# Softmax weights turned in 32x32 blocks by VectorE and through DRAM, in place of TensorE transposes

## The chip, the cores and the metric

The kernel runs on one core of a Trainium2 chip. The metric is the device time of one execution in microseconds, the median of several runs. The kernel before takes 755.2 us (754.77 to 755.24 in three runs). TensorE, VectorE (DVE in the rows), ScalarE (ACT), GpSimd (POOL) and SyncE (SP) each work through a queue of their own, in order, and wait for each other on semaphores; a DMA is issued by one of these queues and runs on the core's 16 DMA engines.

## What is computed

One layer of a hybrid encoder over two batches, of 1024 and of 512 tokens, 1024 wide. An RMS norm and one input projection feed three mixers: latent attention with 4 heads, centred pooling, and gated linear attention. Each mixer's output is multiplied by the SiLU of its gates, the three are joined, projected by `w_out` and added to the input; a last RMS norm follows. The change is in the attention:

```python
def attend(blk):
    qn, qr = blk
    s = (jnp.einsum('bqhd,bkhd->bhqk', qn, k_nope, preferred_element_type=jnp.float32)
         + jnp.einsum('bqhr,bkr->bhqk', qr, k_rope, preferred_element_type=jnp.float32))
    p = jax.nn.softmax(s * MLA_SCALE, axis=-1)
    return jnp.einsum('bhqk,bkhd->bqhd', p.astype(v.dtype), v)
```

## The kernel before

All products of float32 operands are made as three products of a high and a low part (`product`: high x high, high x low, low x high), both parts in the type fp32r. A split is a copy to fp32r (high) and a subtraction (low).

The program has three phases that pass through the same five queues: `phase_front` (norm, input projection, pooling, linear attention), `phase_mla_attend` (attention), `phase_output` (gates, output projection, last norm). The attention has 4 heads x 12 query tiles of 128 = 48 steps (`STEPS`). A tile of the long batch meets 1024 keys (8 blocks of 128, "long"), one of the short batch 512 ("short"); the first eight tiles of a head are long, the last four short. The work is written as a hand-made software pipeline: every engine runs the loop `for m in range(STEPS + GATHER_LAG)` and does in iteration m the scores of tile m and later stages of earlier tiles, by the constants `TURN_LAG, VALUES_LAG, OUTPUT_LAG, GATHER_LAG = 2, 4, 5, 6`:

- TensorE, `scores(m)`: five products per 512 keys into PSUM banks 0 to 3 (two tiles in turn).
- VectorE: the row's maximum (`a_top`) and from it `a_bias`; ScalarE: the exponential into `a_weights` in SBUF, with its sum.
- TensorE, `turn(m)` (line 1994), two steps later: eight or four 128x128 transposes into banks 4 and 5.
- ScalarE takes the high part `a_turned_hi` from there, VectorE subtracts for `a_turned_lo`, a bank of four blocks each time.
- TensorE, `values(p)`, for a pair p of tiles (2p, 2p+1): tokens x turned weights, 24 products of 256 columns for a long pair, 12 for a short one; ScalarE and VectorE split the result (`a_latent_hi`, `a_latent_lo`); TensorE multiplies it by the head's value weights (`output(p)`); VectorE scales it by the reciprocal of the sum and puts it into `mla_mixed` (gather).

In iterations 5, 7 and 9 of a head, `project` makes the next head's queries. In the last head SyncE loads the eight 512 KB rows of `w_out`, GpSimd splits them, and the first tile's mix and gates are made ready; `multiply_first` puts the first tile's mix products between the last steps, `multiply(0, s)` in `phase_output` does the rest of tiles 0 and 1. GpSimd does nothing else in the attention.

## Time and profile before

| | us |
|---|---|
| median of three runs | 755.2 |
| the profiled execution | 754.49 |
| its span | 752.7 |
| TensorE busy | 740.5 |
| VectorE, ScalarE, GpSimd busy | 413.5, 310.1, 219.5 |

The profile is of one execution. Its span runs from the first to the last instruction; 1.8 us of the execution's time lie outside. The busy time of TensorE includes the overlap of products in flight: what one costs is the distance from its start to the next one's. The attention's first product of scores starts at 399.7 us, the output phase's product of tile 1 at 624.2, the last matmul ends at 746.4.

How the rows further down are read. A row of busy time by stretch has the stretch, its length, then busy time and (x instructions) of PE, PEld (TensorE's weight loads, which overlap its matmuls), DVE, ACT and POOL, the granted clock of TensorE as a share of full speed, the mean busy share of the DMA engines and the GB/s that they moved. A row in order of time has start, duration, engine, line, operation, output<-input, shapes and, in brackets, the idle time ahead of it with what ended it. A row of a group has busy time, mean ns of one | idle time ahead of it, with what ended that. A row of DMA issues has KB of one and median us from issue to landing.

### The profile page before, as it was taken

What the parts mean: (1) busy time and instruction counts of PE and PEld (TensorE: products, weight loads), DVE (VectorE), ACT (ScalarE), POOL (GpSimd) and SP (SyncE); (2) the same over time, 40 slices, a digit from 0 to 9 for tenths busy, and PEclk for the clock granted to TensorE, in tenths of its full rate; (3) what the DMA queues carried; (4) which work ended last, traced back from release to release, by engine and by line L of the source; (5) the groups of instructions that cost most, each with busy time, mean ns of one, the idle gap of its engine ahead of it and who ended that gap; (6) DMA issues with size and microseconds to landing.
All of it is one profiled execution on the core that took longest, in us unless ns stands there. A gap on an engine that the chain in (4) does not pass through costs nothing.

```text
span 752.7 us, 14593 instructions
## 1 busy us (share of the span) xinstructions
PE 740.5 (98%) x6024; PEld 625.1 (83%) x6024; DVE 413.5 (55%) x742; ACT 310.1 (41%) x536; POOL 219.5 (29%) x262
## 2 busy tenths in 40 slices
PE   8999999999999999999999999999999999999996
PEld 6997878878888888888887988898898888888885
DVE  6745867376576542026265667667667754433232
ACT  6653544434423422323225545455546643232221
POOL 3223236366556513122400000000009704322320
PEclk9999999999999999999999999999999999999998
DMA  7603021001112133230143000000043035564441
GB/s 255 184 23 88 28 97 57 30 31 40 62 71 88 71 113 118 99 82 13 63 168 112 16 15 14 15 16 15 15 152 128 0 96 177 190 195 151 143 152 56
DMA packets 40623, 64.70 MB, mean 86 GB/s; under 512 B 4434, under 2 KB 23378, under 8 KB 40563
## 3 DMA queue, kind: packets, MB, share of 16 engines
q1 hardware_dynamic: 34272, 49.61, 20.6%
q10 hardware_dynamic: 6290, 14.23, 4.9%
q8 instruction: 45, 0.74, 0.4%
q14 instruction: 16, 0.12, 0.1%
HBM read 43.58 MB, written 19.27 MB: 83 GB/s over the span
## 4 chain that ended last, share of the span: by engine, by line
PE 93%; DVE 3%; ACT 1%; POOL 1%; issue 1%; DMA 0%; DVEq 0%; POOLq 0%
PE psum L78 24%; PE psum L80 23%; PE psum L79 23%; PE psum L1994 5%; PE psum L1521 3%; PE psum L1985 2%; PE psum L1986 2%; PE psum L1360 2%; PE psum L1254 1%; DVE g_state L1062 1%; PE psum L1390 1%; PE psum L1415 1%; PE psum L2014 1%; PE psum L1315 1%; PE psum L1384 1%
## 5 line engine op out<-in xcount | busy, mean ns | idle before, releaser
L78 PE MATMUL psum<-h_hi,z_w_hi 128*128 128x512 f32 x384 | 155.5, 405 | 1.4 <-POOL z_w_lo L805 1.4
L80 PE MATMUL psum<-h_hi,z_w_lo 128*128 128x512 f32 x384 | 149.9, 390 | 0.0
L79 PE MATMUL psum<-h_lo,z_w_hi 128*128 128x512 f32 x384 | 149.8, 390 | 0.0
L78 PEld LDWEIGHTS psum<-h_hi,z_w_hi 128*128 128x128 f32 x384 | 72.1, 188 | 18.0 <-POOL z_w_lo L805 1.8
L80 PEld LDWEIGHTS psum<-h_hi,z_w_lo 128*128 128x128 f32 x384 | 72.1, 188 | 15.6
L79 PEld LDWEIGHTS psum<-h_lo,z_w_hi 128*128 128x128 f32 x384 | 72.2, 188 | 14.3 <-issue 0.7
L78 PE MATMUL psum<-o_w_hi,o_m_hi 128*128 128x512 f32 x184 | 72.6, 394 | 0.0
L80 PE MATMUL psum<-o_w_hi,o_m_lo 128*128 128x512 f32 x184 | 72.3, 393 | 0.0
L79 PE MATMUL psum<-o_w_lo,o_m_hi 128*128 128x512 f32 x184 | 72.2, 392 | 0.0
L1863 ACT ACTIVATE a_weights<-psum,a_bias,mla_q_scale 128x1024 f32<-128x1024 f32 (+1 forms) x48 | 51.1, 1065 | 46.9 <-DVE a_bias L1924 46.7
L805 POOL TENSOR_TENSOR z_w_lo<-z_w_raw,z_w_hi 128x1024 fp32r<-128x1024 f32 x17 | 41.8, 2460 | 95.6 <-ACT z_w_hi L501 93.5
L1812 POOL CAST o_w_hi<-o_w_raw 128x512 fp32r<-128x512 f32 x16 | 9.3, 608 | 194.9 <-DMA o_w_raw<-in_w_out_dram 194.9
L1921 DVE TENSOR_REDUCE a_top<-psum 128x1 f32<-128x1024 f32 (+1 forms) x48 | 50.1, 1043 | 26.8 <-PE psum L1986 26.8
L1877 ACT ACTIVATE a_turned_hi<-psum 128x512 fp32r<-128x512 f32 x80 | 44.2, 596 | 33.7 <-PE psum L1994 32.8
L1076 DVE COPY_PREDICATED g_attn<-g_level_mask,psum 128x256 f32<-128x256 int32 x72 | 32.3, 449 | 38.4 <-ACT g_attn L675 36.3
L1948 DVE TENSOR_TENSOR a_turned_lo<-psum,a_turned_hi 128x512 fp32r<-128x512 f32 x80 | 51.9, 682 | 2.6 <-ACT a_turned_hi L1877 2.6
L2238 DVE TENSOR_TENSOR o_y<-psum,o_x_in 128x512 f32<-128x512 f32 x24 | 16.4, 689 | 53.1 <-PE psum L80 53.1
L80 PE MATMUL psum<-a_turned_hi,mla_tokens_lo 128*128 128x256 f32 x160 | 45.3, 283 | 0.0
L79 PE MATMUL psum<-a_turned_lo,mla_tokens_hi 128*128 128x256 f32 x160 | 45.3, 283 | 0.0
L78 PE MATMUL psum<-a_turned_hi,mla_tokens_hi 128*128 128x256 f32 x160 | 45.2, 282 | 0.0
L514 ACT ACTIVATE z_gate<-psum 128x512 f32<-128x512 f32 x24 | 14.3, 597 | 71.6 <-PE psum L80 71.6
L1994 PE MATMUL psum<-ident,a_weights 128*128 128x128 f32 x320 | 43.6, 275 | 0.0
(252 smaller groups left out, 1520.1 us busy)
## 6 DMA issues: line engine op xcount, KB each, us to landing
z_w_raw<-in_w_z_dram SPq DMA_DIRECT2D x17, 512.0 KB, 3.5
n_x_in<-in_x_dram SPq DMA_DIRECT2D x12, 512.0 KB, 4.1
gates_scratch<-z_gate ACTq DMA_DIRECT2D x24, 256.0 KB, 2.1
o_x_in<-in_x_dram SPq DMA_DIRECT2D x12, 512.0 KB, 3.6
out_dram<-o_y ACTq DMA_DIRECT2D x11, 512.0 KB, 3.2
o_w_raw<-in_w_out_dram SPq DMA_DIRECT2D x8, 512.0 KB, 8.7
rope_scratch<-p_rope_split SPq DMA_DIRECT2D x12, 256.0 KB, 2.6
a_q_rope<-rope_scratch SPq DMA_DIRECT2D x48, 64.0 KB, 1.9
```

Source lines behind the costliest of these rows:

```text
L78: nc.tensor.matmul(out, a_hi, b_hi, start=first, stop=False)
L79: nc.tensor.matmul(out, a_hi, b_lo, start=False, stop=False)
L80: return nc.tensor.matmul(out, a_lo, b_hi, start=False, stop=last)
L805: nc.gpsimd.tensor_tensor(w_lo[:, o % 2, :], raw_of(o)[:, :], w_hi[:, o % 2, :].bitcast(F32), ALU.subtract).then_inc(w_lo_ready, 1)
L1076: nc.vector.copy_predicated(attn[:, t % 2, :, :], level_mask[:, n, :].bitcast(mybir.dt.int32).unsqueeze(1).broadcast_to([P, HEADS, CHUNK]) ...
L1521: mm = nc.tensor.matmul(psum[:, i, part * UNIT:(part + 1) * UNIT], (w_lo if kind == W_LOW else w_hi)[:, o, c], (h_lo if kind == H_LOW else ...
L1863: nc.scalar.activation(weights[:, m % SLOTS, 0:count * P].rearrange("p (a k) -> p a k", k=BLK), psum[:, banks, :], ACT.Exp, bias=bias[:, m ...
L1877: nc.scalar.activation(turned_hi[:, p % 2, 4 * n:4 * n + 4, (tile % 2) * P:(tile % 2 + 1) * P], psum[:, 4 + item % 2, :].rearrange("p (k q ...
L1921: nc.vector.tensor_reduce(top[:, m:m + 1], psum[:, banks, :], mybir.AxisListType.XY, ALU.max)\
L1948: nc.vector.tensor_tensor(turned_lo[at], psum[:, 4 + item % 2, :].rearrange("p (k q) -> p k q", k=4), turned_hi[at].bitcast(F32), ALU.subt ...
L1994: mm = nc.tensor.transpose(psum[:, 4 + item % 2, k * P:(k + 1) * P], weights[:, m % SLOTS, (4 * n + k) * P:(4 * n + k + 1) * P], ident[:, :])
L2238: nc.vector.tensor_tensor(y[:, s, cols], psum[:, 1 - s + 2 * half, :], x_in[:, s, cols], ALU.add)\
```

## The change

- The exponential stays in PSUM (written over the scores). Three pairs of banks hold scores, in place of two.
- VectorE transposes each 32x32 block of the tile from PSUM into `a_spread` in SBUF, arranged by groups of 32 keys. That leaves the partition groups in the wrong place.
- A pass through DRAM exchanges them: ScalarE's queue stores a tile (512 or 256 KB) in iteration m+1, and when both tiles of a pair are stored SyncE issues four loads of 32 partitions each (1 KB or 512 bytes a row) into `a_turned_lo`.
- ScalarE copies that to fp32r for `a_turned_hi` in iterations 2p+3; the low part is subtracted in place, by GpSimd for tiles 0 to 35, 36, 38, 40 and 42, by VectorE for the others.
- The values product comes one step later, so do output and gather. The transposes on TensorE go.
- The next head's queries are made in iterations 8, 9 and 10, in spare banks of the scores.
- The loads of `w_out` are spread over pairs 17 to 22; ScalarE copies the high part of four of its rows (iterations 46 and 48); the mix products of tile 0 stand in iterations 48 and 49, its eight head products in iteration 50 (`multiply_heads`).
- In `phase_front` the first block after the early ones does all products with the weights' high part first and waits for the low part only then.

```diff
@@ TensorE, phase_front.project
+                if i == EARLY and first == 0:
+                    pe.wait_ge(w_hi_ready, o + 1)
...
+                if i == EARLY:
+                    steps = [(HIGH, first, h_hi, w_hi), (H_LOW, first, h_lo, w_hi)]
+                    if last == KT:
+                        steps.append((W_LOW, 0, h_hi, w_lo))
@@ the tables
-TURN_LAG, VALUES_LAG, OUTPUT_LAG, GATHER_LAG = 2, 4, 5, 6
-PROJECT_AT = {5: 0, 7: 1, 9: 2}
+VALUES_LAG, OUTPUT_LAG, GATHER_LAG = 5, 6, 7
+PROJECT_AT = {8: 0, 9: 1, 10: 2}
+W_OUT_LOADS = {17: (4, 5), 18: (6,), 19: (7,), 20: (0, 1), 21: (2,), 22: (3,)}
+W_HI_BY_SCALAR = {46: (0, 1), 48: (2, 3)}
...
+def high_parts_at(m):
+
+    if m % 2 and 1 <= m - 2 < STEPS:
+        return [m - 3, m - 2]
+    return []
@@ SyncE
+            for p in range(PAIRS):
...
+                for n in range(2):
+                    sp.wait_ge(spread_stored[(2 * p + n) % SLOTS], 16 * ((2 * p + n) // SLOTS) + 16)
+                if p >= 2:
+                    sp.wait_ge(values_done, p - 1)
+                for g in range(4):
+                    keys = slice(g * SPREAD, (g + 1) * SPREAD)
+                    sp.dma_start(turned_lo[keys, p % 2, 0:2 * count].bitcast(F32).rearrange("p (x e) -> p x e", x=8),
+                                 rows[p % 3].rearrange("t (a p) (g e) -> g p (t a) e", a=4, g=4)[g])\
+                      .then_inc(turned_loaded[p % 2], 16)
@@ ScalarE
+            def store_spread(m):
+                count, p = keys_of(m), m // 2
+                act.wait_ge(transposed, m + 1)
...
+                act.dma_start(spread_dram[count][p % 3, m % 2], spread[:, m % SLOTS, 0:count])\
+                  .then_inc(spread_stored[m % SLOTS], 16)
...
-                nc.scalar.activation(weights[:, m % SLOTS, 0:count * P].rearrange("p (a k) -> p a k", k=BLK),
-                                     psum[:, banks, :], ACT.Exp, bias=bias[:, m:m + 1],
+                nc.scalar.activation(psum[:, banks, :], psum[:, banks, :], ACT.Exp, bias=bias[:, m:m + 1],
...
+            def take_high(m):
...
+                nc.scalar.activation(turned_hi[part], turned_lo[part].bitcast(F32), ACT.Copy).then_inc(turned_hi_ready, 1)
...
             for m in range(STEPS + GATHER_LAG):
+                if 1 <= m <= STEPS:
+                    store_spread(m - 1)
                 if m < STEPS:
                     exponentials(m)
...
+                for tile in high_parts_at(m):
+                    take_high(tile)
@@ VectorE
+            def transpose(m):
...
+                nc.vector.transpose(spread[:, m % SLOTS, 0:count].rearrange("p (g j e) -> p j g e", g=4, e=SPREAD),
+                                    psum[:, banks, :].rearrange("p b (j g e) -> p (b j) g e", g=4, e=SPREAD))\
@@ GpSimd
+            def take_low(m):
+                pool.wait_ge(turned_hi_ready, m + 1)
+                part = (slice(None), m // 2 % 2, portion(m))
+                nc.gpsimd.tensor_tensor(turned_lo[part], turned_lo[part].bitcast(F32), turned_hi[part].bitcast(F32), ALU.subtract)\
+                  .then_inc(pool_low, 1)
@@ TensorE
-            def turn(m):
...
-                if m >= 2:
-                    pe.wait_ge(exp_done, m - 1)
+                if m >= SLOTS:
+                    pe.wait_ge(transposed, m - 2)
...
+                if m == HEADS_PRODUCTS_STEP:
+                    multiply_heads()
```

How the order of instructions moves, at three places. ScalarE, in the middle of a head's long tiles, before (`a_turned` is the semaphore of TensorE's transposes):

```order
L1877 ACTIVATE a_turned_hi_5117<-psum 128x4x128 [waits a_turned,a_values_done]
L1877 ACTIVATE a_turned_hi_5117<-psum 128x4x128 [waits a_turned]
L1863 ACTIVATE a_weights_5121,a_total_5124<-psum,a_bias_5123,mla_q_scale_67 128x1024 [waits a_turned,a_bias_ready] x2
L1891 ACTIVATE a_latent_hi_5119<-psum 128x256 [waits a_values_done]
L1877 ACTIVATE a_turned_hi_5117<-psum 128x4x128 [waits a_turned] x2
L1877 ACTIVATE a_turned_hi_5117<-psum 128x4x128 [waits a_turned,a_values_done]
L1877 ACTIVATE a_turned_hi_5117<-psum 128x4x128 [waits a_turned]
L1863 ACTIVATE a_weights_5121,a_total_5124<-psum,a_bias_5123,mla_q_scale_67 128x1024 [waits a_turned,a_bias_ready] x2
```

ScalarE at the same place, after (`a_transposed` counts VectorE's block transposes, `a_turned_loaded` the loads of a pair, `a_spread` goes to DRAM):

```order
L1957 ACTIVATE a_turned_hi_5118<-a_turned_lo_5119 128x1024 [waits a_turned_loaded1]
L1937 DMA spread_scratch1024<-a_spread_5122 128x1024 [waits a_transposed]
L1944 ACTIVATE psum,a_total_5125<-psum,a_bias_5124,mla_q_scale_67 128x1024 [waits a_bias_ready]
L1970 ACTIVATE a_latent_hi_5120<-psum 128x256 [waits a_values_done]
L1937 DMA spread_scratch1024<-a_spread_5122 128x1024 [waits a_turned_loaded0,a_transposed]
L1944 ACTIVATE psum,a_total_5125<-psum,a_bias_5124,mla_q_scale_67 128x1024 [waits a_bias_ready]
L1957 ACTIVATE a_turned_hi_5118<-a_turned_lo_5119 128x1024 [waits a_values_done,a_turned_loaded0]
L1957 ACTIVATE a_turned_hi_5118<-a_turned_lo_5119 128x1024 [waits a_turned_loaded0]
L1937 DMA spread_scratch1024<-a_spread_5122 128x1024 [waits a_transposed]
```

The exponential no longer waits for TensorE; a store stands ahead of each exponential, and the two high parts of a pair stand after every second one, ahead of the next store.

VectorE, long tiles, before:

```order
L1943 RECIPROCAL a_share_5125<-a_total_5124 128x1 [waits a_exp_done]
L1948 TENSOR_TENSOR a_turned_lo_5118<-psum,a_turned_hi_5117 128x4x128 [waits a_turned_hi_ready] x2
L1921 TENSOR_REDUCE a_top_5122<-psum 128x1 [waits a_scores_done]
L1924 TENSOR_SCALAR a_bias_5123<-a_top_5122,mla_q_scale_67 128x1 [waits a_top_ready]
L1943 RECIPROCAL a_share_5125<-a_total_5124 128x1 [waits a_exp_done]
L1948 TENSOR_TENSOR a_turned_lo_5118<-psum,a_turned_hi_5117 128x4x128 [waits a_turned_hi_ready] x2
L1921 TENSOR_REDUCE a_top_5122<-psum 128x1 [waits a_scores_done]
```

VectorE at the same place, after:

```order
L2016 TENSOR_REDUCE a_top_5123<-psum 128x1 [waits a_scores_done]
L2019 TENSOR_SCALAR a_bias_5124<-a_top_5123,mla_q_scale_67 128x1 [waits a_top_ready]
L1997 STREAM_TRANSPOSE a_spread_5122<-psum 128x8x4x32 [waits a_spread_stored1,a_exp_done]
L2032 RECIPROCAL a_share_5126<-a_total_5125 128x1
L2016 TENSOR_REDUCE a_top_5123<-psum 128x1 [waits a_scores_done]
L2019 TENSOR_SCALAR a_bias_5124<-a_top_5123,mla_q_scale_67 128x1 [waits a_top_ready]
L2024 COPY a_share_row_74<-psum 128x256 [waits a_output_done]
```

The low part of the turned weights is gone, and between one tile's bias and the next tile's maximum stands the block transpose, which waits for that tile's exponential and for a free slot of `a_spread`.

ScalarE, at the end of the last head, after (tiles 42 to 46; `o_first_step` counts GpSimd's steps on the first tile's mix and gates):

```order
L1957 ACTIVATE a_turned_hi_5118<-a_turned_lo_5119 128x1024 [waits a_values_done,a_turned_loaded1]
L1957 ACTIVATE a_turned_hi_5118<-a_turned_lo_5119 128x1024 [waits a_turned_loaded1]
L1907 ACTIVATE o_first_hi_75<-o_mix_first_73 128x512 [waits o_gate_turned,o_first_step]
L1937 DMA spread_scratch512<-a_spread_5122 128x512 [waits a_transposed]
L1944 ACTIVATE psum,a_total_5125<-psum,a_bias_5124,mla_q_scale_67 128x512 [waits a_bias_ready]
L1970 ACTIVATE a_latent_hi_5120<-psum 128x256 [waits a_values_done]
L1902 ACTIVATE o_gate_first_72<-o_gate_first_72 128x512 [waits o_first_step]
L1913 ACTIVATE o_w_hi0_95<-o_w_raw0_79 128x512 [waits w_out_loaded0]
L1913 ACTIVATE o_w_hi1_96<-o_w_raw0_79 128x512
L1913 ACTIVATE o_w_hi2_97<-o_w_raw1_80 128x512 [waits w_out_loaded1]
```

The copy of the first mix stands between the high parts of tiles 42 and 43 and the store of tile 45; four copies of output weights stand between the exponentials of tiles 46 and 47.

## Rows read from the trace of the kernel before

**Rows 1.** Busy time by stretch: one whole head of the attention
```profile
432.65:486.72 54.07, 54.07 (x351) 48.17 (x349) 37.36 (x77) 28.00 (x53) 0.00 (x0) 1.00 0.06 15
```

**Rows 2.** TensorE, instructions in order of time, 480 to 492 us
```profile
480.03 0.40 PE L78 MATMUL psum<-mla_ckv_hi,a_q_hi 128*128 128x512 f32 x1
...
483.68 0.28 PE L78 MATMUL psum<-a_turned_hi,mla_tokens_hi 128*128 128x256 f32 x1
...
486.56 1.04 PE L1994 MATMUL psum<-ident,a_weights 128*128 128x128 f32 x8
```

**Rows 3.** The page's costliest groups: the transposes of the weights
```profile
L1994 PE MATMUL psum<-ident,a_weights 128*128 128x128 f32 x320 | 43.6, 275 | 0.0
```

**Rows 4.** VectorE and ScalarE in order of time, the first tile
```profile
402.34 1.23 DVE L1921 TENSOR_REDUCE a_top<-psum 128x1 f32<-128x1024 f32 x1 [1.12 <-PE psum L1986]
403.60 0.22 DVE L1924 TENSOR_SCALAR a_bias<-a_top,mla_q_scale 128x1 f32<-128x1 f32 x1
403.85 1.21 ACT L1863 ACTIVATE a_weights<-psum,a_bias,mla_q_scale 128x1024 f32<-128x1024 f32 x1 [3.35 <-DVE a_bias L1924]
404.95 0.19 ACT L1863 ACTIVATION_READ_ACCUMULATOR a_weights<-psum,a_bias,mla_q_scale 128x1 f32 x1
```

**Rows 5.** Groups by line and form, VectorE, 400 to 612 us
```profile
L1937 DVE TENSOR_TENSOR a_latent_lo<-psum,a_latent_hi 128x256 fp32r<-128x256 f32 x23 | 9.8, 424 | 24.6 <-ACT a_latent_hi L1891 24.6
```

**Rows 6.** ScalarE and its DMA queue in order of time, 178 to 180 us
```profile
178.52 0.60 ACT L514 ACTIVATE z_gate<-psum 128x512 f32<-128x512 f32 x1 [4.67 <-PE psum L80]
178.53 0.35 ACTq L547 DMA_DIRECT2D gates_scratch<-z_gate  x1
179.01 1.05 ACT L501 ACTIVATE z_w_hi<-z_w_raw 128x1024 fp32r<-128x1024 f32 x1
```

**Rows 7.** Groups by line, GpSimd, whole span
```profile
L805 POOL TENSOR_TENSOR z_w_lo<-z_w_raw,z_w_hi 128x1024 fp32r<-128x1024 f32 x17 | 41.8, 2460 | 95.6 <-ACT z_w_hi L501 93.5 <-DVE n_x_norm L1107 2.1
L1817 POOL TENSOR_TENSOR o_w_lo<-o_w_raw,o_w_hi 128x512 fp32r<-128x512 f32 x16 | 20.3, 1290 | 0.0
```

**Rows 8.** DMA issues alone in 736:745, 178:182, 115:125; KB, us to landing
```profile
out_dram<-o_y ACTq DMA_DIRECT2D x1, 512.0 KB, 2.6
...
gates_scratch<-z_gate ACTq DMA_DIRECT2D x1, 256.0 KB, 2.1
...
z_w_raw<-in_w_z_dram SPq DMA_DIRECT2D x1, 512.0 KB, 3.3
```

**Rows 9.** Busy time by stretch: DMA engines full, 512-byte rows, then 4 KB
```profile
559.00:560.00 1.00, 1.00 (x8) 0.83 (x7) 0.23 (x1) 0.00 (x0) 0.00 (x0) 1.00 1.21 339
...
565.00:568.00 3.00, 3.00 (x19) 2.57 (x18) 2.15 (x5) 1.89 (x5) 3.00 (x5) 1.00 1.03 408
```

**Rows 10.** ScalarE, VectorE, TensorE in order of time, 615 to 625 us
```profile
615.88 1.28 ACT L2164 ACT_TABLE_LOAD   x1
...
619.31 1.06 ACT L2164 ACTIVATE o_gate_second<-o_gate_second 128x1024 f32<-128x1024 f32 x1 [2.15 <-DMA o_gate_second<-gates_scratch]
...
621.84 0.63 ACT L2171 ACTIVATE o_m_hi<-mla_mixed 128x512 fp32r<-128x512 f32 x1 [1.47 <-POOL mla_mixed L2127]
...
622.51 1.10 DVE L2224 TENSOR_TENSOR o_m_lo<-mla_mixed,o_m_hi 128x512 fp32r<-128x512 f32 x1 [4.19 <-ACT o_m_hi L2171]
...
624.21 0.40 PE L78 MATMUL psum<-o_w_hi,o_m_hi 128*128 128x512 f32 x1
```

**Rows 11.** Busy time by stretch: around TensorE's last matmul
```profile
746.00:748.00 2.00, 0.38 (x2) 0.00 (x0) 0.69 (x1) 0.72 (x2) 0.06 (x1) 1.00 0.00 0
748.00:750.00 2.00, 0.00 (x0) 0.00 (x0) 1.21 (x2) 0.00 (x0) 0.68 (x2) 0.71 0.00 0
```

**Rows 12.** TensorE in order of time, 56 to 60 us
```profile
58.65 0.50 PE L78 MATMUL psum<-h_hi,z_w_hi 128*128 128x512 f32 x1 [1.39 <-POOL z_w_lo L805]
```

**Rows 13.** VectorE in order of time, 632 to 648 us
```profile
634.44 2.30 DVE L2244 SCALAR_TENSOR_TENSOR o_y<-o_y,o_rstd,o_g_row 128x1024 f32<-128x1024 f32 x1 [3.45 <-POOL o_rstd L2142]
...
640.89 1.28 DVE L2244 SCALAR_TENSOR_TENSOR o_y<-o_y,o_rstd,o_g_row 128x1024 f32<-128x1024 f32 x1
```

334 lines of the change are left out of this document (193 added, 141 removed).

## The prediction

> **What bounds the kernel now.** I read the busy shares by stretch first. In one head of the attention (12 query tiles, 54.07 us) TensorE is busy all of the time at the full granted clock, VectorE 37.4 us and ScalarE 28.0 us of it, GpSimd not at all, and the DMA engines 6% [rows 1]. So TensorE's own work sets the head, and the reader is to see that the other queues have room on paper. Then the order of TensorE's work: from 480.03 to 483.68 stand 16 products over 512 columns, 0.228 us each, and from there to 486.56 stand 24 over 256 columns, 0.12 us each [rows 2]. The transposes that the change removes hold TensorE for 43.6 us in all, 10.9 us a head [rows 3]. A long pair of tiles (8 key blocks) is left with 20 x 0.228 + 24 x 0.12 + about 0.6 for the output product = 8.0 us of TensorE, a head with some 43 us in place of 54.
>
> **What replaces them.** A tile's weights now go through seven hands: exponential on ScalarE, block transpose on VectorE, a store on ScalarE's queue, four loads on SyncE's queue, the high part on ScalarE, the low part on GpSimd, the values product. Each hand has time; what I have to ask is whether two of them form a circle. They form two.
>
> **Circle 1, through DRAM.** The order of ScalarE's instructions shows it: store of tile 2p+2, exponential, high parts of tiles 2p and 2p+1, and only then the store of tile 2p+3. The two high parts wait for the loads of pair p, and the loads of pair p+1 wait for the store of tile 2p+3. So one pair cannot take less than: one high part, a store, the loads. The price of each:
> - High part over 1024 columns out of SBUF: a ScalarE copy of that size takes 1.05 us, and the next starts some 0.1 earlier: 0.95. A DMA issue on ScalarE's queue starts together with the copy ahead of it (178.52 and 178.53) [rows 6], so only the first of the two high parts is in the circle. That is a choice: were both in it, it would be 0.95 longer.
> - Store of 512 KB: 2.6 us from issue to landing, 256 KB 2.1 [rows 8].
> - SyncE's wake-up: 0.1, an estimate.
> - Loads: a load of 0.52 MB alone takes 3.3 us [rows 8]; at the 408 GB/s of full DMA engines with 4 KB rows [rows 9] 1.3 of these are data, 2.0 are fixed. The new rows are 1 KB, which no stretch shows full; 512-byte rows ran at 339 GB/s [rows 9]. I take 360, between them: 1.05 MB in 2.9 us (2.6 to 3.1 by the ends). In the same time the store of the next tile is under way, another 0.52 MB, 1.3 us. Loads: 2.0 + 2.9 + 1.3 = 6.2 us. Ends: 4.6 if the store falls beside them and the rate is the higher, 7.5 if reads and writes disturb each other.
>
> Sum for a long pair: 0.95 + 2.6 + 0.1 + 6.2 = 9.9 us. With a short tile's store in it 9.2; a short pair (half the bytes) 0.5 + 2.1 + 0.1 + 4.2 = 6.9.
>
> **Circle 2, VectorE and ScalarE.** VectorE's order per tile is now maximum, bias, block transpose; the transpose waits for the exponential of the same tile, and the maximum of the next tile is queued behind it. From maximum to exponential 1.51 us, exponential with its sum 1.29 [rows 4], the transpose, and 0.1 for two handovers. The trace has no block transpose. Below I bound it by the maximum over the same 1024 elements of PSUM, 1.23 us, above by the longest VectorE row over 1024, 2.30 us [rows 13]; I take 1.23, as it is the row that reads the same banks. A tile: 4.13; a pair with the low part of the latents (0.42 [rows 5]): 8.7 us. (The Trainium skill, Vector Engine (DVE) Microarchitecture Reference, section 3.8 on the reshape front-end, says that the 32x32 array is pipelined to one element per cycle and lane, so an estimate from that page would be little over the maximum's time, and the sum would be the same; no run here shows it yet.)
>
> So circle 1 sets long pairs at 9.9, circle 2 the pairs in which short tiles are loaded while long ones are computed, 8.7. Neither is under TensorE's 8.0. GpSimd has two low parts of 2.46 us a pair [rows 7] and is no bound; they are late, but SyncE and ScalarE don't wait for them. TensorE waits for them at the values product, in one idle block of 2 us a pair, with nothing but its own later work queued behind.
>
> **When the pairs end.** First maximum at 402.34 [rows 4]; exponential done 405.1, transpose 406.4, second tile 4.1 later 410.6; store 413.2; loads 419.5. From there to the loads of pair 21: 11 pairs of 9.9, 4 of 9.2, 3 of 6.9, 3 of 8.7 = 192.5, that is 612.0. The weights of the output product, 4.2 MB, are now loaded between these; 10 us of DMA time in six gaps, of which I let 2 us through: 614.0.
>
> **The last pairs.** Counted from these loads (0). High parts 0 to 2, low part on GpSimd 1.0 to 3.5, two multiplications of the gates to 5.5; ScalarE's copy of the first mix, which stands ahead of the store of tile 45, waits for that (5.5 in place of 1.0). VectorE is behind the same copy, so tile 46 has its exponential at 8.8; then 2.4 us of weight copies on ScalarE; tile 47's exponential 13.1, transpose 13.8, store 15.9, loads 19.8, high parts 20.9. GpSimd's last splits of the output weights, 4 x 2 x 1.29 [rows 7] and the gates, end at 23.4; TensorE waits for them and does the eight products of tile 0 (5.5, to 28.9), values and outputs of the last two pairs (to 34.9). Tile 1 then needs a table load of 1.28, the gates' Silu and GpSimd's multiplication (619.31 to 621.84, 2.5), a copy of 0.63 and a split of about 0.7 [rows 10], partly beside the last output: product of tile 1 at 39. Before, it starts at 624.21 [rows 10]. Now: 614.0 + 39 = 653.0, later by 28.8.
>
> **The rest.** From tile 1's first product to the last matmul 746.4 - 624.2 = 122.2, then 6.3 to the end of the span, both unchanged. The reordered first products after the early blocks wait for the high half alone: the 1.39 us wait at 58.65 goes [rows 12]; behind it TensorE is busy, so it is worth 1.4. The clock: it stood at 1.00 in 746 to 748, in which the last matmul ended, and at 0.71 (partly at the lower level of 1.2 GHz) in the next two microseconds [rows 11]. TensorE will wait 3.6 and 4.2 us in the last pairs and 2 us in each pair; within the pairs its slack of 1.9 covers a slower start, at the end I add 2.0 (ends 0 and 5.5, the eight products at half speed). Sum: 752.7 + 28.8 - 1.4 + 2.0 = 782.1 of span; with the profiled execution's 1.8 outside its span 783.9; the median of the runs shown lies 0.7 above that execution: 784.6, so **785 us**.
>
> **A rule that bears on it.** At 634.44 a VectorE instruction with two SBUF inputs took 2.30 us beside a GpSimd multiplication, and 1.28 at 640.89 without one [rows 13]. (The Trainium skill, SBUF — State Buffer, section "SBUF: two separate sides", calls the shared port pair an exclusive lock between GpSimd and VectorE instructions with two SBUF inputs; by that rule the trace agrees.) The 40 new low parts on GpSimd read SBUF, but VectorE's work in the first three heads reads PSUM; only its eight low parts in the last head meet them, 1 us each at most, of which the last may count: within the range.
>
> **Rivals.**
> 1. The loads are hidden (the store beside them costs nothing, fixed parts overlap): circle 2 sets all long pairs at 8.7. 11 x 1.2 + 4 x 0.5 = 15 less, last pairs 4 less: **766**. For it: the DMA engines have 5.6 us of data in 9.9. Against: every load and store alone already makes 8.3.
> 2. The transpose runs at the upper bound, 1.07 longer a tile: circle 2 is 10.8. 11 x 0.9 + 4 x 1.6 + 3 x 2.1 + the tail's 2: **809**. Reads and writes that disturb each other (loads 7.5) give about the same, 805.
> 3. On the other side: TensorE stays the bound. It does if a pair's circles are both under 8.0, that is the loads under 4.3 us and the transpose under 0.9. Then 43.6 goes, the longer fill (some 5) and last pairs (some 14) give back 19: **730**. For it: in a head TensorE is busy all of the time [rows 1], and the removed work is its own. Against: the prices above; it decides at 8.0 us a long pair. Break-even with before is at about 8.3.
> 4. The clock stays at its lower level during the heads: TensorE needs 16 us a pair and becomes the bound: about 870. Against: two microseconds of waiting near 58 left it at 1.00; a slow TensorE has no more waits.
>
> **Chances.** My forecast 0.46, rival 1 0.20, rival 2 0.13, rival 3 0.17, rival 4 0.01, about equal to before 0.03. Below and above 0.2% (about what a measurement of this kernel can tell from no change): faster 0.17, same 0.03, slower 0.80. The range, which holds forecast and rivals 1 and 2: 757 to 813.
>
> **What the profile after would show.** Right: TensorE at 80 to 85% in the heads, waiting at the first values product for GpSimd's low part; ScalarE's high part waiting for the loads of a_turned_lo; long pairs 9.9 us apart; loads landing 6 us after the store; in the last pairs a wait of the mix copy for GpSimd. Wrong: ScalarE waiting for the bias instead (rival 1 or 2, told apart by the transpose's duration), or TensorE without waits (rival 3). What would break the forecast: a DMA issue that runs ahead of both high parts (a pair 0.95 shorter, 14 us in all), or loads of 1 KB rows well off 360 GB/s.

## The result, and the profile after

The changed kernel takes **822.4 us** (817.9 to 823.2 in four runs) against 755.1: ratio 1.088 (1.087 to 1.090). The prediction said 785, with 757 to 813 as the range. It had the sign and not the size: 67 us lost where 30 were forecast.

The profiled execution took 821.9, its span 820.1. One whole head, from the first maximum to the next head's, answers to [rows 1]; columns as there:

```profile
462.60:524.00 61.40, 48.83 (x270) 41.79 (x269) 35.90 (x70) 26.83 (x45) 24.70 (x13) 0.94 0.60 184
```

54 us have become 61.4, TensorE is busy for 80% of them, and the DMA engines, at 6% before, stand at 60%. On the page, in place of the transposes of [rows 3], stand VectorE's transposes and GpSimd's low parts ("..." marks lines left out):

```profile
L1849 POOL TENSOR_TENSOR a_turned_lo<-a_turned_lo,a_turned_hi 128x1024 fp32r<-128x1024 f32 (+1 forms) x40 | 80.9, 2041 | 183.2 <-ACT a_turned_hi L1957 183.2
...
L1997 DVE STREAM_TRANSPOSE a_spread<-psum 128x1024 f32<-128x1024 f32 (+1 forms) x48 | 51.4, 1070 | 65.0 <-ACT psum L1944 64.8
...
L2104 PE MATMUL psum<-ident,a_share 128*128 128x128 f32 x48 | 11.9, 338 | 58.5 <-DVE a_latent_lo L2035 58.5
```

Most of TensorE's waiting in the attention (58.5 us) is at one instruction, the first of an output product, for the low part of the latents; I had put it at the values product, which waits for a low part of the weights once, for 7.8 us. What stands behind it all is in the chain of work that ended last, here through two long pairs (start, us, what):

```profile
482.88 2.62 DMA spread_scratch<-a_spread
485.50 0.02 SPq L1813
485.52 0.03 issue
485.55 0.30 SPq L1816
...
486.88 6.80 DMA a_turned_lo<-spread_scratch
493.68 0.02 issue
493.71 0.01 ACT a_turned_hi L1957
493.71 2.61 DMA spread_scratch<-a_spread
...
497.72 6.78 DMA a_turned_lo<-spread_scratch
504.50 0.02 issue
504.52 0.01 ACT a_turned_hi L1957
504.53 2.62 DMA spread_scratch<-a_spread
```

Store, four issues, loads, store: no engine computes in this chain. ScalarE in order of time shows how the circle closes:

```profile
493.71 1.06 ACT L1957 ACTIVATE a_turned_hi<-a_turned_lo 128x1024 fp32r<-128x1024 f32 x1 [3.29 <-DMA a_turned_lo<-spread_scratch]
493.71 0.33 ACTq L1937 DMA_DIRECT2D spread_scratch<-a_spread  x1
494.67 1.05 ACT L1957 ACTIVATE a_turned_hi<-a_turned_lo 128x1024 fp32r<-128x1024 f32 x1
495.62 1.16 ACT L1944 ACTIVATE psum<-psum,a_bias,mla_q_scale 128x1024 f32<-128x1024 f32 x1
```

The store of the odd tile starts together with the first high part, 0.03 us behind the landing of the loads at 493.68. It stands behind two high parts in the order and is delayed by neither, but it is delayed by their wait.

Where the time went, by VectorE's maxima of tiles 0, 36 and 47 (402.34 in [rows 4], the others from the same view). Before:

```profile
559.77 1.22 DVE L1921 TENSOR_REDUCE a_top<-psum 128x1 f32<-128x1024 f32 x1 [0.98 <-PE psum L1986]
...
604.23 0.68 DVE L1921 TENSOR_REDUCE a_top<-psum 128x1 f32<-128x512 f32 x1
```

After:

```profile
400.89 1.23 DVE L2016 TENSOR_REDUCE a_top<-psum 128x1 f32<-128x1024 f32 x1 [1.04 <-PE psum L2080]
...
587.03 1.23 DVE L2016 TENSOR_REDUCE a_top<-psum 128x1 f32<-128x1024 f32 x1 [3.21 <-PE psum L2080]
...
656.95 0.68 DVE L2016 TENSOR_REDUCE a_top<-psum 128x1 f32<-128x512 f32 x1
```

e13, in the last column, is the run without the pass and without the low parts of the first three heads (see the experiments).

| us | before | after | e13 |
|---|---|---|---|
| start to tile 0 | 402.3 | 400.9 | 401.1 |
| tile 0 to 36, three heads | 157.4 | 186.1 | 151.0 |
| tile 36 to 47, last head | 44.5 | 69.9 | 53.9 |
| tile 47 to the end of the span | 148.5 | 163.2 | 163.5 |
| span | 752.7 | 820.1 | 769.5 |

### The profile page after: what moved, and what is told of

It is laid out like the page before. It is cut to its first block, busy times and chain, and to the rows that moved or that the text cites. A ratio compares the mean times of both kernels' runs of the same rounds, so it can differ in the third digit from the quotient of the medians.

```text
span 820.1 us, 14085 instructions
## 1 busy us (share of the span) xinstructions
PE 731.5 (89%) x5704; PEld 608.6 (74%) x5704; DVE 419.2 (51%) x718; ACT 309.8 (38%) x512; POOL 299.1 (36%) x294
## 4 chain that ended last, share of the span: by engine, by line
PE 65%; DMA 19%; DVE 4%; ACT 3%; SPq 3%; POOL 3%; issue 2%; DVEq 0%; POOLq 0%; ACTq 0%
PE psum L78 18%; PE psum L80 17%; PE psum L79 17%; DMA a_turned_lo<-spread_scratch 14%; DMA spread_scratch<-a_spread 5%; PE psum L1535 4%; SPq L1816 3%; PE psum L1374 2%; PE psum L1254 1%; DVE g_state L1062 1%; PE psum L1404 1%; PE psum L1429 1%; ACT psum L1944 1%; ACT a_turned_hi L1957 1%; DVE a_spread L1997 1%
## 5 line engine op out<-in xcount | busy, mean ns | idle before, releaser
L78 PE MATMUL psum<-h_hi,z_w_hi 128*128 128x512 f32 x376 | 152.4, 405 | 0.0
L1849 POOL TENSOR_TENSOR a_turned_lo<-a_turned_lo,a_turned_hi 128x1024 fp32r<-128x1024 f32 (+1 forms) x40 | 80.9, 2041 | 183.2 <-ACT a_turned_hi L1957 183.2
L80 PE MATMUL psum<-h_hi,z_w_lo 128*128 128x512 f32 x376 | 146.7, 390 | 0.0
L79 PE MATMUL psum<-h_lo,z_w_hi 128*128 128x512 f32 x376 | 146.6, 390 | 0.0
L1997 DVE STREAM_TRANSPOSE a_spread<-psum 128x1024 f32<-128x1024 f32 (+1 forms) x48 | 51.4, 1070 | 65.0 <-ACT psum L1944 64.8
L78 PEld LDWEIGHTS psum<-h_hi,z_w_hi 128*128 128x128 f32 x376 | 70.6, 188 | 15.9 <-issue 0.7
L1944 ACT ACTIVATE psum<-psum,a_bias,mla_q_scale 128x1024 f32<-128x1024 f32 (+1 forms) x48 | 49.4, 1029 | 85.6 <-DVE a_bias L2019 83.2
L1957 ACT ACTIVATE a_turned_hi<-a_turned_lo 128x1024 fp32r<-128x1024 f32 (+1 forms) x48 | 41.3, 907 | 63.1 <-DMA a_turned_lo<-spread_scratch 63.1
L2104 PE MATMUL psum<-ident,a_share 128*128 128x128 f32 x48 | 11.9, 338 | 58.5 <-DVE a_latent_lo L2035 58.5
L2016 DVE TENSOR_REDUCE a_top<-psum 128x1 f32<-128x1024 f32 (+1 forms) x48 | 49.5, 1032 | 13.1 <-PE psum L2080 13.1
L2104 PEld LDWEIGHTS psum<-ident,a_share 128*128 128x128 f32 x48 | 5.8, 161 | 66.3 <-DVE a_share L2032 63.1
L78 PEld LDWEIGHTS psum<-o_w_hi,o_m_hi 128*128 128x128 f32 x184 | 35.5, 193 | 16.0 <-issue 7.9
```

Of the source, the lines that this page charges most:

```text
L78: nc.tensor.matmul(out, a_hi, b_hi, start=first, stop=False)
L79: nc.tensor.matmul(out, a_hi, b_lo, start=False, stop=False)
L80: return nc.tensor.matmul(out, a_lo, b_hi, start=False, stop=last)
L1849: nc.gpsimd.tensor_tensor(turned_lo[part], turned_lo[part].bitcast(F32), turned_hi[part].bitcast(F32), ALU.subtract)\
L1944: nc.scalar.activation(psum[:, banks, :], psum[:, banks, :], ACT.Exp, bias=bias[:, m:m + 1], scale=keep.q_scale[:, tile:tile + 1], accum_o ...
L1957: nc.scalar.activation(turned_hi[part], turned_lo[part].bitcast(F32), ACT.Copy).then_inc(turned_hi_ready, 1)
```

## The experiments

Times are medians; ratios are to runs of the kernel before on the same chip, with their 95% interval. A store counts from its issue to its last landing, the loads from the first issue to the last landing; a pair's time is the distance between the last landings of its loads and of the loads before. Differences of under 5 us between two kernels are to be read with care: the changed kernel's own four runs lie between 817.9 and 823.2. In the cuts of code "..." marks lines left out.

### What the pass costs

**No low part.** GpSimd's subtraction left out:

```diff
@@ GpSimd
-            for m in range(LAST_HEAD):
-                take_low(m)
@@ TensorE, values, first three heads
-                pe.wait_ge(pool_low, sum(m <= tiles[1] for m in POOL_LOW))
+                pe.wait_ge(turned_hi_ready, tiles[1] + 1)
```

> GpSimd's low parts of the turned weights are left out for the first three heads (tiles 0 to 35); the values products take the loaded weights themselves for the low part, so the output is not the reference's. Theory A: the low parts (4.7 us for the two of a long pair) are late for TensorE alone, and a long pair's loads don't wait for its values; 822 less 0 to 4: 820. Theory G: the first long loads behind short tiles (465.55, 526.94 and 590.19, each about 3 us behind the landing of the store) wait for a values product that waits for the low part; then 3 such waits go and the chain behind each is shorter: 812 or less.

Measured 820.6, ratio 1.086 (1.085 to 1.088) against 1.088 (1.087 to 1.090) of the changed kernel. 66.7 us of GpSimd work between 425 and 590 us are gone and nothing clear of the noise follows: they were off the path, as theory A had it.

**No pass, first form.** ScalarE takes the high part from `a_spread` two steps later, no store, no loads, shorter lags:

```diff
-VALUES_LAG, OUTPUT_LAG, GATHER_LAG = 5, 6, 7
+VALUES_LAG, OUTPUT_LAG, GATHER_LAG = 3, 4, 5
...
-                nc.scalar.activation(turned_hi[part], turned_lo[part].bitcast(F32), ACT.Copy).then_inc(turned_hi_ready, 1)
+                nc.scalar.activation(turned_hi[part], spread[:, m % SLOTS, 0:keys_of(m)], ACT.Copy).then_inc(turned_hi_ready, 1)
```

> The pass through DRAM is left out: VectorE's block transposes stay, ScalarE and GpSimd take high and low part from their output in SBUF, two tiles later, and values, output and gather come two steps earlier than in the changed kernel. The partition groups are not exchanged, so the output is not the reference's. Theory A (the pass is what costs): VectorE's loop of 4.34 us a long tile and some 2.9 a short one is left, 32 x 4.34 + 16 x 2.9 = 185 us from 401, then some 30 us of last steps, so tile 1 at about 616 to 624 and the end at 752 (744 to 762). Rival: with the transposes gone TensorE is the bound and the time falls by most of their 43.6 us, 730 or less.

817.7, ratio 1.083 (1.081 to 1.084): both theories missed. I took it for a wait of the experiment's own making and moved latents, output and gather one step back (`LATENT_LAG`, `OUTPUT_LAG`, `GATHER_LAG` = 4, 5, 6):

> As the run without the pass through DRAM, but latents, output and gather one step later behind the values, because there VectorE stood at the latents' low part (490.13, idle 3.07) with the next maximum behind it, and TensorE's values waited for the gather. The output is again not the reference's (no exchange of partition groups). Theory A (the pass is what costs, the run before it had a wait of its own making): 752 (744 to 762). Rival H (the hands around the pass are as slow as the pass: TensorE waits for low parts and latents whatever their source): over 795.

837.4, ratio 1.110 (1.108 to 1.112), worse still. VectorE in order of time shows why:

```profile
490.79 1.25 DVE L1985 STREAM_TRANSPOSE a_spread<-psum 128x1024 f32<-128x1024 f32 x1 [1.36 <-ACT psum L1932]
491.97 0.12 DVE L2020 RECIPROCAL a_share<-a_total 128x1 f32<-128x1 f32 x1
498.25 1.23 DVE L2004 TENSOR_REDUCE a_top<-psum 128x1 f32<-128x1024 f32 x1 [6.17 <-PE psum L2068]
```

With a lag of 3 the low part is made right before the values product that needs it (TensorE idle 4.09 us for it at 489.89), and the next scores stand behind that product; so VectorE idles 6.2 us for scores. The lag of five steps had hidden the low parts, as the run without them shows. The time is over rival H's 795, but by waits that the shorter lags made. Neither run measures the pass.

**No pass, same lags.** The transposes write three pairs' places and everything stands in its old step, on top of the run without low parts:

```diff
-                if m >= SLOTS:
-                    dve.wait_ge(spread_stored[m % SLOTS], 16 * (m // SLOTS))
-                nc.vector.transpose(spread[:, m % SLOTS, 0:count].rearrange("p (g j e) -> p j g e", g=4, e=SPREAD),
+                if m >= 6:
+                    dve.wait_ge(values_done, m // 2 - 2)
+                nc.vector.transpose(turned_lo[:, m // 2 % 3, portion(m)].rearrange("p (g j e) -> p j g e", g=4, e=SPREAD),
```

> As the run without low parts in the first three heads, and the pass through DRAM left out as well: VectorE's block transposes write the place of the loaded weights (three pairs of it), ScalarE takes the high parts from there, and every step stands in the iteration in which it stands in the changed kernel. The output is not the reference's (no exchange, no low parts). Beside the 820.6 of the run without low parts this leaves the pass alone as the difference. Theory A (the pass is what costs): VectorE's loop of 4.4 us a long tile and 2.9 a short one, 401 + 187 + 33 = 621 for tile 1, 752 (744 to 762) at the end. Rival H (in-order waits of TensorE around the pass cost as much without it, as the two runs without exchange and with shorter lags would have it, 817.7 and 837.4): over 790.

771.4, ratio 1.022 (1.020 to 1.023). Against the 820.6 of its partner the pass through DRAM costs **49 us**; and without pass and low parts the kernel is still 16 slower than before. Neither forecast had this: theory A said 744 to 762, rival H over 790. The pass is about three quarters of the loss (49 of 67), not all of it. A head takes 50.5 us there:

```profile
451.10:501.60 50.50, 47.16 (x270) 40.70 (x269) 36.15 (x69) 26.88 (x45) 0.00 (x0) 0.97 0.06 16
```

The transposes freed 10.9 us of TensorE in a head, and with a free exchange 3.5 of them come out (50.5 in place of 54.0). The table above shows the rest: three heads 6.4 faster, last head 9.4 and everything behind it 15.0 slower.

### The loads

**Neighbouring rows, and rows of 4 KB.** The loads' source alone is changed:

```diff
-                 rows[p % 3].rearrange("t (a p) (g e) -> g p (t a) e", a=4, g=4)[g])
+                 rows[p % 3].rearrange("t q (r e) -> (t q r) e", r=4).rearrange("(x g p) e -> g p x e", x=8, g=4)[g])
```

> The four loads of a pair read the same number of rows of 1 KB (512 bytes for short tiles), but rows that lie next to each other in DRAM in place of every fourth one; the weights then reach the wrong partitions, so the output is not the reference's. In the changed kernel a 1 KB packet of the loads takes 65 ns in the mean and 46 in the median. Theory D (the stride of 4 KB in DRAM slows the reads): loads of a long pair 6.3 in place of 8.1, 18 long pairs, about 30 us less, 792. Theory E (size of rows, four issues in a row and the store beside them make the 8.1): within 4 us of 822.

```diff
-                for g in range(4):
-                    keys = slice(g * SPREAD, (g + 1) * SPREAD)
...
+                for n in range(2):
+                    sp.dma_start(turned_lo[:, p % 2, n * count:(n + 1) * count].bitcast(F32), rows[p % 3][n])
```

> The pair is loaded by two transfers of 128 partitions with rows of 4 KB (2 KB for short tiles) in place of four with rows of 1 KB; the same bytes, but without the exchange of partition groups, so the output is not the reference's. Theory E (small rows and four issues cost it): first row in flight 1.0, two times 1.3 of data, 1.3 of the next store and some 1 to land: 5.9 us in place of 8.1; 18 pairs, 40 us less, 782 +- 6. Theory F (the reads wait for the rows just written, or for the latency of DRAM, whatever their size): loads still over 7.5 and the time over 812.

809.1, ratio 1.072 (1.070 to 1.074), and 785.1, ratio 1.039 (1.037 to 1.042). The distance of the rows costs 0.6 us of a long pair's loads (8.1 to 7.5 in the mean of eight), not the 1.8 of theory D; neither theory had the time of 809.1 (792 and 818 to 826), of which the rows' distance makes some 11 in 18 pairs. With rows of 4 KB 5.0 to 5.7 are left, 2.4 to 3.1 less, and the time is in theory E's range (776 to 788). But that comparison is not of the rows alone: the last issue comes 0.41 us behind the first in place of 1.35, and only 0.23 to 0.30 MB of the next store lie beside the loads where it was all of its 0.52. Rows' size, number of issues and the store beside are not told apart by a run; the account below takes them from the queues' busy time.

**Rows joined.** The same exchange with the small pieces on the store's side:

```diff
-                act.dma_start(spread_dram[count][p % 3, m % 2], spread[:, m % SLOTS, 0:count])
+                home = spread_dram[count][p % 3].rearrange("t q n -> (t q n)")\
+                    .rearrange("(g p t a e) -> t a p g e", g=4, p=SPREAD, t=2, a=4)
+                for a in range(4):
+                    act.dma_start(home[m % 2, a], spread[a * SPREAD:(a + 1) * SPREAD, m % SLOTS, 0:count].rearrange("p (g e) -> p g e", g=4))
```

> The same exchange by another layout in DRAM: the store writes pieces of 1 KB (four issues of 32 partitions each), so that the load of a pair is one transfer whose row of 8 KB a partition lies in one piece. Theory E (many small rows and issues on the load's side make it 8.1): loads 5.0 to 5.6 as with rows of 4 KB; the store 3.6 with four issues in place of 2.6; 1.6 us a pair less, 18 pairs, 793 +- 6. Rival: the small pieces cost the same on whichever side they are, 815 or more.

804.6, ratio 1.067 (1.064 to 1.069), 18 us less than the changed kernel, where 787 to 799 and for the rival 815 or more had been expected. The chain through two long pairs:

```profile
482.05 2.42 DMA spread_scratch<-a_spread
...
484.53 6.07 DMA a_turned_lo<-spread_scratch
...
491.97 2.36 DMA spread_scratch<-a_spread
...
494.38 6.01 DMA a_turned_lo<-spread_scratch
```

The load falls from 8.1 to 6.0 (I had said 5.0 to 5.6), the store with its four issues takes 3.7 for 2.6. A long pair takes 9.85, the 1.0 less that 2.1 and 1.1 make.

### The order of the queues

**Store ahead of the high parts.**

```diff
-    if m % 2 and 1 <= m - 2 < STEPS:
-        return [m - 3, m - 2]
+    if m % 2 == 0 and 1 <= m - 3 < LAST_HEAD:
+        return [m - 4, m - 3]
+    if m % 2 and LAST_HEAD < m - 2 < STEPS:
+        return [m - 3, m - 2]
```

> ScalarE takes the two high parts of a pair one iteration later, behind the store of the pair's next odd tile and the exponential after it (first three heads; the last head as in the changed kernel). In the changed kernel every store of an odd tile starts within 0.1 us of the landing of the loads before it, and a long pair takes 10.8 us: store 2.6, loads 8.1. Theory A, a loop through the store: store and loads follow each other because the store stands behind ScalarE's wait for the loads; without that the loop runs over two pairs and the next limit is 8.4 to 9.0 us a pair: 18 pairs, about 25 us less, 797 +- 6. Theory B, the transfers fill the DMA engines: store and loads then lie on top of each other and each takes longer, a pair stays over 10.3 us and the time over 812.

802.7, ratio 1.064 (1.062 to 1.066): 20 us less, by order alone, within what theory A said. It holds for the loop, with a part of theory B in it: long pairs take 8.4 to 10.7 us (12.0 behind short tiles, as before), the odd tile's store now lies on the loads and takes 4 to 6 in most pairs where it took 2.6, the loads 8.4 where they took 8.1.

**Maximum ahead of the transpose.**

```diff
             for m in range(STEPS + GATHER_LAG):
-                if m < STEPS:
-                    tile, _, count = QUERY_TILES[m % TILES]
...
+                if m + 1 < STEPS:
+                    find_bias(m + 1)
```

> VectorE finds the maximum and bias of tile m+1 ahead of the block transpose of tile m. Theory A (a pair is bound by store and loads): VectorE is not what a long pair waits for, the store of the odd tile still starts at the landing of the loads; 822 +- 4. Theory C (VectorE's and ScalarE's loop of maximum, exponential and transpose has a part in the pair): 1.5 us less a tile in the stretches where it binds, 810 or less.

858.2, ratio 1.137 (1.128 to 1.147): 36 us more, which neither theory had. VectorE at the start of the second head:

```profile
472.68 1.24 DVE L1997 STREAM_TRANSPOSE a_spread<-psum 128x1024 f32<-128x1024 f32 x1
473.85 0.12 DVE L2036 RECIPROCAL a_share<-a_total 128x1 f32<-128x1 f32 x1
473.89 0.40 DVE L2039 TENSOR_TENSOR a_latent_lo<-psum,a_latent_hi 128x256 fp32r<-128x256 f32 x1
478.87 1.23 DVE L2011 TENSOR_REDUCE a_top<-psum 128x1 f32<-128x1024 f32 x1 [4.58 <-PE psum L2084]
480.13 0.21 DVE L2014 TENSOR_SCALAR a_bias<-a_top,mla_q_scale 128x1 f32<-128x1 f32 x1
480.26 1.24 DVE L1997 STREAM_TRANSPOSE a_spread<-psum 128x1024 f32<-128x1024 f32 x1
```

and TensorE there:

```profile
474.44 0.40 PE L2108 MATMUL psum<-ident,a_share 128*128 128x128 f32 x2 [3.97 <-DVE a_latent_lo L2039]
```

The transpose at 480.26 has its exponential long since and stands behind a maximum that waits 4.6 us for TensorE's next scores. So the store waits for TensorE. TensorE had waited 4.0 us for the low part of the latents, which VectorE makes only at 473.89, behind a maximum and a block transpose of its own, and the scores stand behind that. The chain that ends last holds no transfer from 470 to 485 us, only VectorE and TensorE: a new circle, of these two.

**Output one step later.** `OUTPUT_LAG, GATHER_LAG = 7, 8`.

> Output and gather one step later: on TensorE the values of pair q now stand ahead of the output of pair q-1. In the changed kernel TensorE waits for the low latents at that output (458.12, idle 2.72), runs at the lower clock behind it, and the values of pair 3 end at 465.3; the loads of pair 5, whose store landed at 462.70, are issued at 465.55, right behind. If this is why the first long loads after short tiles are 3 us late: 3 such waits go, 8 us less, 814 +- 3. Rival: these loads then wait for something else (the low part of that pair, ready at 458.8, leaves room), 820 or more.

820.1, ratio 1.085 (1.083 to 1.087). Of the three waits of 3 us two shrink to 0.4 and 0.5 and one stays at 2.5, but the long pair behind each takes 13.1, 13.6 and 13.4 in place of 12.1, 12.0 and 13.9: the odd tile's store starts 1.9 and 2.4 us behind the landing of the loads in the first two, where it had been 1.2 and 0.4. The time is the rival's. The wait was real and in two of the three places had another limit right behind it.

**Mix copy later**: `split_first` and its subtraction at `SPLIT_FIRST_STEP + 1`.

> ScalarE's copy of the first mix and VectorE's subtraction stand one iteration later, behind the store of tile 45 and the exponential of tile 46. In the changed kernel the copy waits 3.5 us for GpSimd (651.29) and the store with it, though the loads of pair 21 landed at 645.82. If that wait is on the path to the end (my step on the last pairs): the store comes 5.4 us earlier, the copies of output weights 3 to 5, and with them GpSimd's last splits: 3 to 5 us less, 818. If GpSimd's own splits set the end by themselves: nothing, 822.

817.8, ratio 1.083 (1.082 to 1.085), 4.6 less. The number is the expected one, the reason is not. ScalarE at the landing of the loads of pair 21, in the changed kernel and in this one:

```profile
645.84 2.00 ACT L1957 ACTIVATE a_turned_hi<-a_turned_lo 128x1024 fp32r<-128x1024 f32 x2 [5.43 <-DMA a_turned_lo<-spread_scratch]
```

```profile
641.01 1.06 ACT L1957 ACTIVATE a_turned_hi<-a_turned_lo 128x1024 fp32r<-128x1024 f32 x1 [5.99 <-DMA a_turned_lo<-spread_scratch]
```

The profiled execution is 5.2 us shorter (814.9 of span), and 4.8 of them are there before the first reordered instruction. From that landing to the end it takes 173.9 in place of 174.3: the store of tile 45 does start at the landing and the product of tile 1 comes 1.7 us earlier, but the output phase takes 1.3 of them back. The 4.8 lie for the most part where the loads of pairs 5, 11 and 17 wait behind the landing of their store: 1.3, 1.6 and 1.7 us here, 2.8, 3.1 and 3.1 in the changed kernel, by the same code. Why these waits differ is not shown. So the reordering is worth 0.4 in these traces, and the agreement with 818 is luck.

**Together.** The store's order with the mix copy; both with the later output; both with the joined layout:

> High parts behind the next store and the mix copy behind the store of tile 45, without the later output: the two gains of 19.7 and 4.6 lie in different stretches and add, 798 +- 2. If the run with three orders (805.4) was slow by the mix copy and not by the later output, this one is over 802.

> The changed kernel with three changes of order at once: high parts behind the next store, mix copy behind the store of tile 45, output one step later. If the gains add: 20 + 5 + 8 = 33 less, 789 +- 4. If the first and the third remove the same wait: 797.

> The layout with one load a pair, high parts behind the next store in the first three heads, mix copy behind the store of tile 45. The layout gave 17.8, the two orders 19.7 and 4.6. If they add (the loads' length and the loop are separate): 822.4 - 42 = 780. If a pair is then at the limit of VectorE's loop, 8.7: the layout's pairs of 9.85 can give 1.15 each in 14 pairs, 16 more, and 5: 784. If ScalarE's eight store issues a pair take its time from the exponentials: 795 or more.

802.7 (ratio 1.061 to 1.064), 805.4 (1.065 to 1.069), 806.4 (1.067 to 1.072). Nothing adds. The mix copy had nothing to add (above), and with the later output it is 2.7 more, not less. Layout and early store together still take 9.3 to 9.9 us for most long pairs; their limit is shown below, with the filled wait.

**The clock.** With the store ahead of the high parts (e1) the chain goes through TensorE, too: it waits some 2 us for the low latents, then its scores run at a lower granted clock (stretches of that kernel, columns as in [rows 1]):

```profile
469.00:471.50 2.50, 0.31 (x2) 0.02 (x1) 1.91 (x5) 1.91 (x5) 1.31 (x2) 1.00 0.26 82
471.50:475.00 3.50, 3.49 (x12) 2.91 (x13) 2.10 (x3) 1.30 (x2) 1.20 (x1) 0.57 0.92 252
475.00:479.00 4.00, 4.00 (x23) 3.52 (x23) 2.60 (x6) 1.32 (x3) 0.00 (x0) 0.95 0.70 257
```

So I filled the wait with products that nothing uses, in that kernel, in the changed one and in the joined layout:

```diff
+                if p:
+                    pe.wait_ge(gathered, 2 * p)
+                for _ in range(16 if p < 3 * TILES // 2 else 0):
+                    nc.tensor.matmul(psum[:, 7 - p % 2, PAIR:], keep.tokens_hi[:, 0, :], keep.ckv_hi[:, 0:PAIR], start=True, stop=True)
```

> The kernel with high parts behind the next store (802.7), and on TensorE 16 extra products over 256 columns (1.9 us) into a free bank ahead of each output of the first three heads, where it waits 1.9 to 2.6 us for the low latents in most pairs; nothing uses them. In that kernel the chain that ends last goes through TensorE: scores at 0.43 us a product in place of 0.23 for 3.3 us behind each such wait (granted clock 0.57 there, 1.00 before), then the maximum. Theory K (the clock that falls in the wait costs the chain 1.6 us a pair): 10 to 12 pairs of the 18 gain it, 783 to 788. Rival: the products only add work, 1 us a pair where the wait was short, 802 to 812.

> The changed kernel with the same extra products. There the chain of a long pair is store and loads and doesn't go through TensorE; only the stretch behind each head's short tiles does (458.12 to 465.3). Theory K: 1.5 us at each of the three, 818 +- 2. If the clock costs every pair something: 805 or less. If the extra products delay values and with them the loads: over 824.

> The layout with one load a pair and high parts behind the next store, with the extra products. Without them (and with the mix copy later) 806.4, where shorter loads and the early store gave no more together than each alone. Theory K says why: both had met the same limit, TensorE's scores behind a wait at the lower clock; with the clock kept up 785 +- 6. Rival: their limit is ScalarE with eight store issues a pair, over 800.

807.4 (ratio 1.068 to 1.071), 818.7 (1.083 to 1.090), 805.8 (1.066 to 1.071). The clock stayed up, and in the first and the third the time did not fall; in the second it is the 818 of theory K, but its interval overlaps the changed kernel's, and of the three waits of the loads that it was to shorten two fall just as much in the run with the later mix copy, without a filler. One head of the first of them:

```profile
513.10:568.90 55.80, 55.69 (x358) 50.43 (x357) 35.50 (x67) 25.97 (x43) 22.15 (x12) 1.00 0.69 198
```

TensorE is busy for all of it at full clock: six times 1.91 us of filler, 11.5, take the room of the waits and of the slower scores (TensorE busy 47.7 of 55.8 us there without them). The chain there is TensorE's alone. This is no test of theory K for that kernel, since it set a new bound in place of the one it took away; a shorter filler was not tried.

For the joined layout with the early store it says more. In the second head the granted clock is 1.00 (480 to 502 us), and the chain goes through ScalarE all the same, 31% of it through its issuing of stores:

```profile
489.05 2.80 ACTq L1940 DMA_DIRECT2D spread_scratch<-a_spread  x4
491.90 1.18 ACT L1947 ACTIVATE psum<-psum,a_bias,mla_q_scale 128x1024 f32<-128x1024 f32 x1 [4.16 <-issue]
```

The bias of that exponential was ready at 490.43; the exponential stands behind the four issues of a store, which end at 491.85 (2.8 us here, 1.8 in most places). Two stores a pair make eight issues, and the high parts of the pair come on top. In the same kernel without the filler the largest single part of the chain from 425 to 590 us is again these issues, 20%. In the third head with the filler the chain lies mostly on TensorE, filler included, as in the first of the three runs. So ScalarE with eight issues a pair, on record as the rival for both runs, holds a large part of this kernel's chain, and with the clock kept up it still does.

### The reordered front

The kernel before with this part of the change alone:

```diff
-                    pe.wait_ge(w_lo_ready, o + 1)
+                    if i != EARLY:
+                        pe.wait_ge(w_lo_ready, o + 1)
@@
+                if i == EARLY:
+                    steps = [(HIGH, first, h_hi, w_hi), (H_LOW, first, h_lo, w_hi)]
+                    if last == KT:
+                        steps.append((W_LOW, 0, h_hi, w_lo))
```

> The kernel before with one part of the change alone: the first block of the projection after the early ones takes all products with the high part of the weights first and waits for the low part only then. My step: the wait of 1.39 us at 58.65 goes and TensorE is busy behind it: 1.4 us less than before, 753.7. Rival: the time comes back at a later wait of the front phase, and nothing is left, 755.1.

754.0, ratio 0.999 (0.998 to 1.000): 1.0 less, at the edge of what these runs tell. The wait at 58.65 is gone in its trace. In the changed kernel tile 0's maximum comes at 400.89, 1.45 earlier than in [rows 4], in others with the same front at up to 401.66, 0.7 earlier. It is a small gain, if it is one.

## Why the prediction was off

The times of the steps, in the prediction's order.

- **Circle 1, the high part.** "High part, 0.95, only the first of the two is in the circle": it measures nothing. The issue of a DMA that stands behind two activations starts with the first of them, once that one's wait is over. I had the row for it, [rows 6], and counted one copy too many. -0.95. The prediction had named this as one of two things that would break it.
- **Circle 1, the store.** 2.6 said, 2.61 measured.
- **Circle 1, the loads.** 6.2 said, 8.1 measured. This is the step that failed. I took one price for the start (2.0) and a rate of 360 GB/s for 1 KB rows, between the ends of [rows 9]. The end of the range, 7.5, did not hold it either. The queues of the changed kernel from 496 to 505 us, with the loads issued at 496.37 and the store beside them (packets, MB, share of the 16 engines' time):

```profile
q1 hardware_dynamic: 1088, 1.05, 46.5%
q10 hardware_dynamic: 144, 0.52, 15.1%
```

  The loads' 46.5% of 9 us is 4.2 us for 1.05 MB: 250 GB/s in place of 360, and 1.3 us more than the 2.9 said. The store takes 1.4, said 1.3. The first row starts 0.9 behind the issue and the landing comes 0.8 behind the last row, 1.7 together, said 2.0. The rest of the 8.1, some 0.8, is time in which the engines have nothing to move, while the issues come one by one (the fourth 1.35 us behind the first). So the term that was mis-sized is the rate for 1 KB rows, and one was left out, the spacing of the four issues.

  With rows of 4 KB (run e4, 483 to 489 us) the same 1.05 MB take 59.5% of 6 us, 3.6; the distance of the rows made 0.6. The trace does not show that the store's traffic disturbs the loads, as the second rival had it: over five long pairs a 1 KB packet of the loads took 62 ns in the mean beside a packet of the store and 68 without one. Why the mean lies so far over the median of 46 stays open. The prediction had named "loads of 1 KB rows well off 360 GB/s" as the other thing that would break it.
- **A long pair.** 9.9 said; six long pairs without a short tile's store (in three of them 0.26 MB for the next head's queries follow the loads) take 10.89, 10.51, 10.84, 10.81, 10.65 and 10.48, mean 10.7. Over 11 pairs 8.8 us. With a short store in it 10.06 for 9.2, over four pairs 3.4; short pairs 6.8 for 6.9.
- **SyncE's wake-up.** 0.1 said, an estimate without a row; 0.05 measured (485.50 to 485.55).
- **Circle 2.** The transpose takes 1.25, said 1.23. (By the rule of the Trainium skill, Vector Engine (DVE) Microarchitecture Reference, section 3.8, the trace agrees.) But the three pairs that I gave to this circle, 8.7 each, take 10.3, 12.0 and 14.2, 2.3 of the last beside the loads of `w_out`. What sets them is a third circle, which I did not look for: the loads wait for the values product of the pair before last, that one stands on TensorE behind the output product, and that waits for latents whose high part stands on ScalarE behind the wait for the loads. TensorE at that place:

```profile
458.12 0.66 PE L2104 MATMUL psum<-ident,a_share 128*128 128x128 f32 x2 [2.72 <-DVE a_latent_lo L2035]
458.43 0.56 PE L78 MATMUL psum<-a_latent_hi,mla_w_v_hi 128*128 128x256 f32 x1
```

  In the chain ahead of it stand, from the landing of the loads at 452.99: the high parts, the exponential, the high part of the next head's queries, and on VectorE the block transpose and the low latents. Behind it the scores run at a granted clock of 0.50 (458 to 461 us), then come the values.

  The store of pair 5 had landed at 462.70, its loads were issued at 465.55. In the prediction TensorE's idle block had "nothing but its own later work queued behind"; that work was the scores and the values for which others wait. 8.1 us in these three pairs (without the loads of `w_out`), and 4.1 in the three behind them: two take 12.1 and 12.0, the third 13.9 beside loads of `w_out`, counted here as 12.1. This is one execution; with the waits of the run with the later mix copy it would be some 4 less.
- **The loads of the output weights.** Held against the pairs one head earlier (11 to 15), pairs 17 to 21 are 7.6 longer; I let 2.0 through. 5.6.
- **First pair.** Loads 421.6, said 419.5: the loads' 1.7 and a store that took 4.5.
- **The last pairs.** Said 39 from the loads of pair 21 to the product of tile 1, measured 645.82 to 690.18, 44.4. Most steps came within 0.3: the copy waiting for GpSimd 5.5 (5.5 said), tile 46's exponential 8.8 (8.8), tile 47's 13.0 (13.1), store 15.7 (15.9), loads 20.1 (19.8); the splits 24.2 (23.4). Then the eight products took 8.4 for 5.5, because 14 of their 24 products ran at half clock (670 to 676: granted 0.50), and the last two pairs' values and outputs 7.2 for 6.0. I had 2.0 for the clock in a line of its own.
- **Behind.** 123.6 from tile 1 to the last matmul, said 122.2: its first seven products again at half clock, 7 x 0.2.

The sum: 2.1 + 8.8 + 3.4 - 0.3 + 8.1 + 4.1 + 5.6 + 5.4 + 1.4 - 0.6 (front and clock, entered apart) = 38.0, the 820.1 of span against 782.1. About a third of it is the size of the loads, a third the third circle with what follows it, and a third the other traffic, the clock and the last pairs.

Of the rivals the first, loads fully hidden, was put at 766; with the pass (and the low parts of three heads) really gone it is 771.4. That the sums agree fits the prices of circle 2, the tail and the fill, but does not show each of them: the chain in e13 goes through TensorE's products for 55% of a head, and the product of tile 1 comes at 639.4, not at the 634 that rival 1 means. The larger part of the error lies in the pass and in what waits around it. The second rival's price for disturbed transfers, 805, was the nearest, with a reason that the trace does not bear out. Rival 4 leaned on two microseconds of waiting near 58; that was one wait of 1.39 [rows 12], and behind the wait of 2.72 at 458.12 the granted clock was 0.50 from 458 to 461 us.

That early store, joined layout and both together end at 803 to 806 has not one reason. With the joined layout alone store and loads still follow each other, 9.85 a long pair; with both ScalarE's eight issues are the largest part of the chain. What stays open is the floor of the early store alone: its chain goes over VectorE, ScalarE and TensorE (from 425 to 590 us the loads make 4.5% of it, 49% in the changed kernel), in part through scores at the lower clock, and how much the clock costs there the filled run could not show. Open too is what makes the waits of pairs 5, 11 and 17 differ between runs of the same code, and how the loads' time divides between rows' size, issues and the store beside them.

## What to carry to other kernels

A transfer's wait on an in-order queue is a wait for everything behind it: ask of each wait which issue stands behind it, and whether that issue starts the next transfer. If it does, the pipeline has a circle however many buffers it has; here moving one store ahead of one wait gave back 20 us of 67. Freed time of the bounding engine is only worth what the next loop leaves (3.5 of 10.9 us a head here, with a free exchange), and an experiment that takes a step out must keep the lags, or it measures its own new waits. And a gain of the expected size is looked up in the trace: it has to lie behind the instruction that was moved.

## What the runs showed of the hardware

- A pair's loads of 1 MB of 1 KB rows 4 KB apart took 8.1 us in four issues with a 0.5 MB store beside them, 7.5 with neighbouring rows, 5.0 to 5.7 as two transfers with rows of 4 KB, 6.0 as one with 8 KB a partition, the last two with about half of a store beside them. (The Trainium skill, DMA: Bandwidth & Descriptors, section on the measured bandwidth, has 6.15 us for 1 MB into 128 partitions, issued from GpSimd. That is the time in which the DMA engines are busy, without the issue. Counted so, from the first row to the end of the last, the load of 8 KB a partition took 4.7 to 4.8 us, well under that figure, and the 1 KB rows with the store between them 6.1 to 6.8.)
- An issue of a DMA on SyncE's or ScalarE's queue mostly took 0.3 to 0.5 us, four in a row 1.8, and an activation queued behind them on ScalarE waited for their end (491.85 and 491.90 in the joined layout with the filled wait).
- The store of tile 1 lands 4.5 to 4.8 us after its issue in every kernel here that stores a tile in one issue, with no other data beside most of it, where others of its size land after 2.6. The transfers of 405 to 414 us hold one instruction load among the stores (queues: packets, MB, share):

```profile
q10 hardware_dynamic: 301, 1.10, 30.9%
q8 instruction: 1, 0.02, 0.7%
```

  In the trace it took 0.97 us, from 411.46 to 412.43; 15 of the store's 16 completions came between 411.48 and 411.65 and one at 413.58, and the store's last row of 4 KB starts at 412.42, as the instruction load ends. That it held that row up is the likely reading; no run here takes it away.
- After a wait of 2 to 3 us TensorE's granted clock stood at or near the lower level of 1.2 GHz: 0.57 from 471.5 to 475 in the kernel with the early store, behind 2.2 us of idling, and 0.50 from 670 to 676 in the changed kernel, behind 3.0; with the wait filled by products it stayed at 1.00 for a whole head.
